# A two-block transformer in fp32 on one core: norms and the last units of each output projection taken by token tile

## The reference, cut to what matters

```python
def first_block(x, mem, ...):            # one even layer, one odd layer
    mem_n = rmsnorm(mem, mem_norm_g)
    h = even_layer(x, ...)               # rmsnorm, w_in, pool mixer + retention + memory attention, silu gate, w_out
    h = odd_layer(h, ...)                # rmsnorm, w_in, compressed/selected/window attention + memory attention, w_out
    return rmsnorm(h, final_g)

def second_block(x, p, ...):
    for i in range(2):
        h = rmsnorm_2(x, norm_mix[i])    # na_q, na_k, na_v, q_lat, kv_lat, k_rope, gate_a, gate_b = h @ w_in[i]
        ...                              # neighbourhood and latent attention
        x = x + merged @ w_out[i]
        x = x + expert_choice_moe(rmsnorm_2(x, norm_moe[i]), w_router[i], ...)   # 16 experts, 32 tokens each
        ple_gate = jax.nn.sigmoid(rmsnorm_2(x, norm_ple[i]) @ ple_gate_w[i])
        x = x + ple_gate * (p[i] @ ple_w[i])
    return rmsnorm_2(x, norm_final)

def rmsnorm(x, g):
    return x * lax.rsqrt(jnp.mean(x * x, axis=-1, keepdims=True) + 1e-6) * g
```

## Time and profile before

| | us |
|---|---|
| median of 3 runs | 2079.78 |
| the profiled execution, its own time | 2083.16 |
| its span | 2081.3 |
| PE busy | 1683.0 |
| PE weight loads busy | 1245.7 |
| DVE busy | 610.6 |
| ACT busy | 496.0 |
| POOL busy | 161.7 |

### The profile page before, as it was taken

One profiled execution on the slowest core, in us unless ns is written; L12 is line 12 of the kernel. 1 busy time (PEld: TensorE's weight loads), 2 busy tenths in 40 slices (PEclk: granted clock), 3 DMA queues, 4 the chain that ended last, 5 costly groups with the idle time before them and its releaser, 6 DMA issues. The chain is left out here.

```text
span 2081.3 us, 30041 instructions
## 1 busy us (share of the span) xinstructions
PE 1683.0 (81%) x12816; PEld 1245.7 (60%) x12816; DVE 610.6 (29%) x884; ACT 496.0 (24%) x884; POOL 161.7 (8%) x170
## 2 busy tenths in 40 slices
PE   7999999998799998866575756899998666757656
PEld 6999899997698777432232323887875232323225
DVE  2645444577344434000000001644342000000004
ACT  3434234455243331000000002432321000000003
POOL 0014000010031010000000001210100000000002
PEclk9999999999999999998899897999998898989997
DMA  8454649332453417899999998544238999999992
GB/s 286 146 167 143 191 143 308 111 102 83 140 147 116 162 53 317 370 426 426 424 426 427 425 427 334 156 123 166 87 155 353 424 427 425 426 426 428 426 419 92
DMA packets 173169, 563.66 MB, mean 271 GB/s; under 512 B 12745, under 2 KB 127327, under 8 KB 140172
## 3 DMA queue, kind: packets, MB, share of 16 engines
q1 hardware_dynamic: 165168, 552.05, 68.6%
q10 hardware_dynamic: 7900, 10.13, 1.5%
HBM read 561.08 MB, written 5.23 MB: 272 GB/s over the span
## 5 line engine op out<-in xcount | busy, mean ns | idle before, releaser
L1357 PE MATMUL bank<-ring,big 128*32 128x256 f32 x3840 | 279.7, 443 | 187.5 <-DMA ring<-in_moe_w 187.4
L886 PE MATMUL bank<-big_r,ring_r 128*128 128x256 f32 (+1 forms) x2880 | 362.4, 287 | 0.2 <-issue 0.2
L886 PEld LDWEIGHTS bank<-big_r,ring_r 128*128 128x128 f32 (+1 forms) x2880 | 353.7, 189 | 1.6 <-issue 1.2
L1357 PEld LDWEIGHTS bank<-ring,big 128*32 128x32 f32 x3840 | 146.5, 124 | 327.4 <-issue 285.7
L1755 DVE TENSOR_TENSOR ring_r<-ring,ring_r 128x2048 fp32r<-128x2048 f32 (+2 forms) x112 | 246.8, 2210 | 184.6 <-ACT ring_r L1439 183.2
L1479 ACT ACTIVATE big<-bank 128x512 f32<-128x512 f32 (+2 forms) x186 | 87.8, 490 | 542.8 <-PE bank L861 335.6
L1439 ACT ACTIVATE ring_r<-ring 128x2048 fp32r<-128x2048 f32 (+2 forms) x116 | 208.5, 1806 | 25.1 <-issue 12.4
L1378 PE MATMUL bank<-ring,big 128*32 128x512 f32 x1024 | 136.8, 628 | 76.5 <-DMA ring<-in_moe_w 59.5
L886 PE MATMUL bank<-ring_r,big_r 128*128 128x256 f32 (+3 forms) x1440 | 181.3, 287 | 1.9 <-POOL ring_r L2175 1.9
L886 PEld LDWEIGHTS bank<-ring_r,big_r 128*128 128x128 f32 x1440 | 178.3, 199 | 3.8 <-POOL ring_r L2175 2.7
L861 PE MATMUL bank<-big 128*128 128x128 f32 (+5 forms) x634 | 111.7, 309 | 70.1 <-ACT big L1429 32.5
(11 more groups left out here) (180 smaller groups left out, 1329.5 us busy)
## 6 DMA issues: line engine op xcount, KB each, us to landing
ring<-in_moe_w SPq DMA_DIRECT2D x120, 2048.0 KB, 23.7
ring<-in_moe_w SPq DMA_DIRECT2D x128, 1024.0 KB, 24.9
ring<-in_w_in SPq DMA_DIRECT2D x30, 1024.0 KB, 5.3
ring<-in_od_w_in SPq DMA_DIRECT2D x22, 1024.0 KB, 5.3
big<-in_moe_w SPq DMA_DIRECT2D x8, 2048.0 KB, 13.3
ring<-in_ev_w_in SPq DMA_DIRECT2D x11, 1024.0 KB, 11.0
ring<-in_ev_w_in SPq DMA_DIRECT2D x12, 768.0 KB, 4.5
ring<-in_od_cmp_w SPq DMA_DIRECT2D x8, 1024.0 KB, 8.4
```

The costliest lines, as they stand in the source:

```text
L886: ins = unit[0].mark(mm(dst, lhsT, rhs, start=start and n == 0, stop=stop and n == len(terms) - 1))
L1357: ins = mm(banks[5 + up][32 * j:32 * j + 32, 0:256], xg[:, k, q, :], wv[:, r, 256 * j:256 * (j + 1)], start=k == 0, stop=k == KC - 1)
```

## The change

There are five parts.

1. **Output projections.** Of each, the last four units (`LAST`) are done for token tile 0, all four, and then for token tile 1. DVE adds tile 0 into x, and its norm runs, while PE is at tile 1. The transposes of tile 0 stand between the units of tile 1 (`first_T`). A unit that is kept for its second tile (`hold`) counts `begun` up only there (`release`). The rounded halves of the gated rows (`g_high`) move to other places in SBUF.
2. **Norms.** Sums, roots, scalings, transposes and high and low parts go by token tile, each with semaphores of its own.
3. **The start of the second block.** One pass forms both norms: DVE multiplies x by `final_g` into `yb`, ACT sums the squares of x and of `yb`, POOL forms both factors (`double_norm`). The layer begins with the `nav` units, which have tokens on the output partitions and so can go by token tile (`values_start`). The unit's low weights are waited for late (`tile_rest`).
4. **The router.** Raw rows of x are transposed and multiplied by the gains, and the exponential takes the norm's factor as its scale. The rows for the gather are scaled afterwards on ACT, in an order in which the gather reads 128 columns in a row.
5. **Embedding gates.** Each evacuation is 512 columns of one token tile in place of 256 columns of both; all four `pg` units are kept for both tiles (`embed_gates`). The unit whose low part POOL makes is `pg` 3 in place of `pg` 1. The output is stored by tile.

Second output projection, PE, before: L1112 is a matmul of `out_proj`, L1070 to L1074 the values of head 11, L861 the transposes, L886 the first projection of layer 0.

```diff
+ODD = (proj("o_mk", 0) + [("T1", 2)] + proj("o_mk", 1) + proj("o_mv", 0) + [("uT", 2)] + proj("o_xq", 0, 1) + proj("o_mv", 1)
        + attention(MH, proj("o_gate", 6, 7) + proj("o_kc", 0) + proj("o_vc", 0) + proj("o_ks", 0))
...
+            k = out.index(("proj", "o_gate", 5))
+            out.insert(k + 1, ("outu", 1, 0))
+            out.insert(out.index(("NT", NH - 2)) + 1, ("outu", 1, 1))
...
+_first = [e for e in LAYER_PLAN if e[0] == "split"][:2]
+LAYER_PLAN = _first + [e for e in LAYER_PLAN if e not in _first]
+LAST = 4
...
+                def hold(s):
+                    s.first = False
+                    return s
+
+                def release(s):
+                    s.first, s.step = True, 2
+                    return s
...
+            def tile_T(t, src):
+
+                for half in range(2):
+                    for k in range(4):
+                        c = (4 * half + k) * P
+                        ins = tr(banks[4 + 2 * t + half][:, k * P:(k + 1) * P], src[:, t, c:c + P])
+                    ins.then_inc(uT_psum, 1)
...
+                    if i < n - LAST:
+                        tile(U, i, 0), tile(U, i, 1)
+                    else:
+                        if held:
+                            U.hold()
+                        held.append(U)
+                        tile(U, i, 0)
+                for k, U in enumerate(held):
+                    if k:
+                        U.release()
+                    if k == (3 if j == 1 else 2):
+                        first_T(l, j)
+                    tile(U, n - LAST + k, 1)
...
+            def tile_product(bank, c0, U, l, j, t, fresh, chunk_waits):
...
+                for k in range(KC):
+                    if chunk_waits:
+                        tile_ready(l, j, t, k)
+                    for x_ in (uTh_r, uT_r):
+                        ins = U.mark(mm(dst, x_[:, k, toks], hi[:, k, :], start=fresh and k == 0 and x_ is uTh_r,
+                                        stop=False, skip_group_check=True))
+                return ins
...
+            def tile_rest(bank, c0, U, t):
+
+                lo, hi = U.parts(256)
+                pe.wait_ge(*U.low)
+                for k in range(KC):
+                    ins = mm(bank[:, c0:c0 + 256], uTh_r[:, k, t * P:(t + 1) * P], lo[:, k, :], start=False,
+                             stop=k == KC - 1, skip_group_check=True)
+                return ins
...
+            def values_start(l):
+
+                held = []
+                for t in range(TT):
...
+                    for i in range(2):
+                        if t == 0:
+                            held.append(Unit(l, ("nav", i), late=True))
...
+                            if i:
+                                held[i].hold()
...
+                            bank = bank_of(l, "nav", i)
+                            if i:
+                                held[i].release()
+                        tile_product(bank, t * T, held[i], l, 0, t, t == 0, i == 0)
+                        ins = tile_rest(bank, t * T, held[i], t)
+                        if t:
+                            ins.then_inc(proj_done, 1)
...
+            def embed_gates(l):
+
+                held = []
+                rows_T(l, 2, 0)
+                for i in range(4):
+                    t, p = i // 2, i % 2
+                    if i == 1:
+                        rows_T(l, 2, 1)
+                    if i == 3 and l + 1 < LAYERS:
+                        rows_T(l + 1, 0, 0)
+                    bank = wait_bank(l, "pg", i)
+                    for n in (2 * p, 2 * p + 1):
+                        if t == 0:
+                            held.append(Unit(l, ("pg", n), late=True))
...
+                                held[n].hold()
+                        elif n:
+                            held[n].release()
+                        tile_product(bank, (n % 2) * T, held[n], l, 2, t, n % 2 == 0, p == 0 and n == 0)
+                        if t:
+                            ins = tile_rest(bank, (n % 2) * T, held[n], t)
+                    if t == 0:
+                        for n in (2 * p, 2 * p + 1):
+                            ins = tile_rest(bank, (n % 2) * T, held[n], t)
+                    ins.then_inc(proj_done, 1)
...
+                            ins = mm(banks[4 + 2 * (k // 4)][:, (k % 4) * P:(k % 4 + 1) * P], u[:, t, k * P:(k + 1) * P],
                                      onehot[:, t].rearrange("p q s -> p (q s)"), start=t == 0, stop=t == TT - 1)
...
+                        act.wait_ge(x_ready, 6)
+                        tile_ss(0, x[:, 0, :], lss)
+                        act.wait_ge(norm_ss[0], norm_at(None, 3) + 1)
+                        act.wait_ge(y_ready, 1)
+                        tile_ss(0, yb[:, 0, :])
+                        split(0, *EARLY[1])
+                        tile_scale(0, 0, 0, yb[:, 0, :])
+                        tile_high(0, 0, 0, layer_gains(0))
+                        act.wait_ge(x_ready, 8)
+                        tile_ss(1, x[:, 1, :], lss)
+                        act.wait_ge(norm_ss[1], norm_at(None, 3) + 1)
+                        act.wait_ge(y_ready, 2)
+                        tile_ss(1, yb[:, 1, :])
...
+                act.wait_ge(x_ready, 4 * out_at(l, 2) + 2)
+                tile_ss(0, x[:, 0, :])
+                tile_raw(l, 0, gl[:, 8:])
+                act.wait_ge(x_ready, 4 * out_at(l, 2) + 4)
+                tile_ss(1, x[:, 1, :])
+                tile_raw(l, 1, gl[:, 8:])
+                evacuate(l, *PLE_W[0][1:])
...
+                    A(aff[:, t, :], banks[3][:, t * NE:(t + 1) * NE], ACT.Exp, bias=rt[:, 6 + t:7 + t],
+                      scale=rstd[:, t:t + 1], accum_out=rt[:, 2 + t:3 + t]).then_inc(rt_exp, 1)
+                for t in range(TT):
+                    A(u[:, t, :].rearrange("p (i r q) -> p i q r", i=2, r=4),
+                      x[:, t, :].rearrange("p (i q r) -> p i q r", i=2, r=4), ACT.Copy,
+                      scale=rstd[:, t:t + 1]).then_inc(u_ready[t], 1)
...
+                        add_out(None, 1, 0)
+                        gained(0)
+                        final_rows(0)
+                        split(0, *EARLY[1])
+                        tile_parts(0, 0, 0, layer_gains(0))
+                        add_out(None, 1, 1)
+                        gained(1)
+                        tile_scale(0, 0, yb[:, 1, :])
+                        final_rows(1)
...
+                tile_ss(x[:, 1, :])
+                tile_parts(l, 2, 0, gl[:, 16:])
+                split(l, "pg", 1)
+                split(l, "pg", 2)
+                tile_parts(l, 2, 1, gl[:, 16:])
+                more = l + 1 < LAYERS
+                evacuate(l, "pg", 0)
+                if more:
+                    split(l + 1, *EARLY[0])
+                evacuate(l, "pg", 1)
+                evacuate(l, "pg", 2)
+                if more:
...
+            def double_norm(t):
+
+                c = slice(t, t + 1)
+                pool.wait_ge(norm_ss[t], norm_at(None, 3) + 1)
+                steps.link(g.tensor_scalar(lms[:, c], lss[:, c], 1.0 / D, EPS, ALU.mult, ALU.add))
+                g.tensor_tensor(lrstd[:, c], lms[:, c], neghalf[:, 0:1], ALU.pow).then_inc(norm_rstd[t], 1)
+                pool.wait_ge(norm_rstd[t], norm_at(None, 3) + 1)
+                pool.wait_ge(norm_ss[t], norm_at(0, 0) + 1)
+                steps.link(g.tensor_tensor(ms[:, c], ss[:, c], lrstd[:, c], ALU.mult))
+                steps.link(g.tensor_tensor(ms[:, c], ms[:, c], lrstd[:, c], ALU.mult))
+                steps.link(g.tensor_scalar(ms[:, c], ms[:, c], 1.0 / D, EPS, ALU.mult, ALU.add))
+                steps.link(g.tensor_tensor(ms[:, c], ms[:, c], neghalf[:, 0:1], ALU.pow))
+                g.tensor_tensor(rstd[:, c], ms[:, c], lrstd[:, c], ALU.mult).then_inc(norm_rstd[t], 1)
```

435 lines of the change are left out of this document (256 added, 179 removed).

## The result

| | before | after |
|---|---|---|
| median of 4 runs, us | 2080.57 | 2049.07 |
| lowest to highest | 2075.74 to 2083.79 | 2044.10 to 2052.04 |
| the profiled execution, own time | 2083.16 | 2051.12 |
| its span | 2081.3 | 2049.3 |
| PE busy | 1683.0 | 1650.9 |

The ratio is 0.9846, 95% interval 0.9830 to 0.9863: 31.5 us faster. The forecast was 2048, range 2038 to 2065.

What follows compares the result with a forecast made beforehand. The weight stream bounds the expert phases, PE's own work the rest, where only its holes can be won. Gains of 5.5 + 2.1 + 11.2 + 0 + 8.9 + 4.1 = 31.8 us give 2048 us, range 2038 to 2065.

Steps and rivals of the forecast that it cites:

- Places 3 and 5: Routers of both layers (T: output projection's start): later first expert load and shorter logits path cancel, 0 us.
- Rival A: Expert phases: the stream's late start is not given back in either layer, 17 us lost, 2065 us; chance 0.08.
- Place 2(c): Second output projection's end to first layer 0 products: kept half units hide the by-tile norm chain, 11.2 us gained.
- Place 2(b): Second output projection, head 11's values and unit 7: waits around the values go, 2.1 us gained.
- Place 2(a): Second output projection's start: low parts made before head 11's scores, unit 0 at 504.8, 5.5 us gained of 8.06.
- Place 4: Experts to layer 1: by-tile norms shorten both norm holes, first product 5.5 us after the experts; 8.9 us gained.
- Place 6: Kernel's end: last embedding gates start by tile, 1.9 us, and a shorter store tail, 2.2 us; 4.1 us gained.
- place 1: First output projection: the odd layer's norm was already hidden and stays hidden by tile, 0 us.
- B: Rival: DVE and ACT become the bound in the holes, halving gains at 2(c) and 4; 2058 us, chance 0.10.
- C: Rival: POOL's split of `pg` 3 blocks DVE for 3 us; 2051 us, or 2054 with the last layer; chance 0.08.
- D: Rival: held units stop SP's loads 8.5 us at five places or more, so the kernel is slower, 2091 us; chance 0.04.
- E: Rival: weights' low parts, not norms, end the holes, so by-tile norms bring nothing at 2(c) and 4; 2068 us, chance 0.04.

Runs made afterwards that it cites:

- the control: The changed kernel unedited, timed again on the same chip as follow-up runs: median 2047.46 us of 5 runs, ratio 0.9828 against the kernel before.
- the first of the two strided runs: The changed kernel with the gather reading every fourth column again and ScalarE scaling rows in plain order; single execution, own time 2049.95 us.

## Why the prediction came out right

**Places 3 and 5, the routers: right, and for the reason given.** The load went out at T + 15.4 (I had 14.65), the stream's idle time was 8.8 us before (8.5), and the phase ended as before to 0.4 us. The first expert stood at T + 47.4, not 49: without the gather the path to it is 3.7 us shorter, where I had 4.2, and the gather, which I counted as nothing, took 5.33 us for 7.74. The run with two kept units shows what the sum of 0 was made of: release the ring as before, and 6.2 us a layer come in. Rival A needed the idle time to stay; it went.

**Place 2(c): right; 10.7 for 11.2.** Beside the matmuls of the projection and of the products I foresaw 3.4 us: measured about 3.5, with 0.8 of transposes at 553.83 and 2.7 at 564. The products themselves took 0.4 us longer than before. Without kept units 8.5 us come back.

**Place 2(b): 2.1 for 2.1.** From unit 0's start to the projection's end, tile 0's transposes left out, 3.9 us were gained. 1.8 of them are the clock's, at units 0 and 1; the rest is head 11's values and the waits around them.

**Place 2(a): the mechanism half right, 3.8 for 5.5.** I saw the 2.5 us at head 10's values (2.76) and took unit 0 to wait for nothing but them, at 504.8. It started at 507.88. One thing was missing from the term: PE may not write to the projection's PSUM banks before VectorE has read head 11's scores, and that read now stands behind two splits. It is what I had as the lower bound, 3.0, "if head 11's steps, late by another split, come back to PE". PE also took 4.05 us for values that take 2.2, at a granted clock of 0.50 after its wait, but this cost nothing: in the three profiles where they took 2.2, PE waited for the same read. The order is worth 4 us, not 5.5. The clock gave some back: unit 0 and 1 took 12.13 us for 13.94, which no term foresaw. So the place as a whole, 18.5 for 18.8, is right in part by luck.

**Place 4: 10.7 for 8.9, and partly luck.** The first product came 5.4 us after the experts, as worked out (5.5). In twelve profiles with the same code here it came after 4.8 to 7.2 us in layer 0, and after 7.2 in the control. One part of that is where the count starts: the last expert's eight matmuls took 1.99 us in the control and 3.65 here. The other part is an encounter that the prediction didn't see. By tile, GpSimd forms tile 0's root while VectorE sums tile 1's squares (L1898, two inputs in SBUF), and whichever begins first holds the other up. Here GpSimd was first, by 0.06 us; in the run with `pg` 1 on GpSimd VectorE was:

```profile
1269.29 0.54 POOL L2396 TENSOR_TENSOR big<-big 128x1 f32<-128x1 f32 x1
1269.35 1.23 DVE L1898 CUSTOM_DVE_ANT_0 big<-big 128x1024 f32<-128x1024 f32 x1
```

```profile
1268.63 1.22 DVE L1898 CUSTOM_DVE_ANT_0 big<-big 128x1024 f32<-128x1024 f32 x1
1268.68 1.57 POOL L2396 TENSOR_TENSOR big<-big 128x1 f32<-128x1 f32 x1
```

An operation on a single column took 1.57 us for 0.54, and ScalarE's scaling of tile 0 waited for it. Of the 24 starts of the gates in the twelve profiles (two layers each), 18 have one of the root's two steps held, for 0.5 or 1.0 us. No run tests an order that avoids it. Counted from the start of the last expert's eight matmuls, the place takes 59.7 us before and 48.7 to 50.0 in the twelve, so 9.7 to 11.0 are gained in each of them. The transposes' wait and the chain of the second norm cost less than the 1.5 us set aside.

**Place 6: 6.0 for 4.1.** The tail after the last product was 9.0 us for 11.8, 2.8 where I had 2.2. The start was put at 1.9. The first product came 4.2 us sooner (5.5 after the last expert for 9.7), and the gates then took 1.0 longer, tile 1's transposes included: 3.2.

**Left out.** The start of the program: two norms stand there with nothing to hide them, and by tile GpSimd makes two roots one after the other. The first transposes begin at 13.94 for 13.54, the second ones at 27.2 for 25.2. In the other executions they began between 25.4 and 28.0, as the 32 matmuls before them took 7.17 to 9.54 us, so most of it is the clock's. And place 1 cost 0.9, cause open. Against these two stood more gain at 4 and 6; that the forecast met the time to 1 us owes something to that.

**Rivals.** B (queues halve the gains): 2(c) and place 4 kept theirs. C (GpSimd's split of `pg` 3 shuts VectorE out): it happened, at another operation and for less. VectorE in the changed kernel, and below it GpSimd:

```profile
1275.38 5.01 DVE L1957 TENSOR_TENSOR ring_r<-ring,ring_r 128x2048 fp32r<-128x2048 f32 x2
...
1283.30 2.13 DVE L2045 SCALAR_TENSOR_TENSOR big<-big 128x512 f32<-128x512 f32 x1
```

```profile
1271.45 4.58 POOL L2422 TENSOR_TENSOR ring_r<-ring,ring_r 128x2048 fp32r<-128x2048 f32 x1
1278.90 5.98 POOL L2422 TENSOR_TENSOR ring_r<-ring,ring_r 128x2048 fp32r<-128x2048 f32 x1 [2.87 <-ACT ring_r L1575]
```

GpSimd's split stretched from 4.58 to 5.98 until VectorE's ended at 1280.39, and then VectorE's gate operation stood until 1284.88: 2.13 us for 0.68. That fits the exclusion told of in the prediction. PE waited 0.85 us at 1293.13 at the end of that queue, 3 us were feared. In layer 0 of the twelve profiles the gate operation took 2.1 to 2.2 us in three, and PE waited 0.85, 0.92 and 0.99 us there; in the nine others it took 0.69 to 0.98, and PE did not wait. So the two go together, though no edit tests it. D (slower): its stalls never came, PE's waits name no DMA in the PE-bound stages. E: the norm's waits did end the holes.

**Signs that were wrong.** Unit 0's start and the first expert's are told of above. PE's busy time was to stay within 1%; it fell by 1.9%, 1683.0 to 1650.9. Nearly all of that is the gather, which the prediction put at nothing because it lay in a hidden stretch. Its 256 matmuls are booked with 61.9 us before and 33.6 after, 28.3 of the 32.1. With the gather alone put back (the first of the two strided runs) it is 61.9 again, and PE is busy for 1676.2. In the expert phase DMA sets the pace, so this work was saved and no time won: a busy sum tells nothing of time where the engine is not the limit.

## What to carry to other kernels

When a stage is bound by a stream of weights, look at what releases its first load, not only at what its first consumer waits for: here a shorter path and a late release cancelled within a microsecond, and releasing early without giving up the short path won 12 us more. When a wait is named after one producer, ask what else must be true at that point (a PSUM bank to be free, here), or the next producer in the queue takes its place. When a step is cut in two, look at which other engine now works beside each half: here VectorE's sum and GpSimd's root met on the critical path. Read small effects between two events near the edit; whole times of one code differed by more than the effect.

## What the hardware showed beyond that

- Behind a hole PE's work often ran at half speed. Head 10's first values took 1.19 us for 0.69 after the wait of 2.76, at a granted clock of 0.50; eight transposes took 1.97 for 1.03 after one of 4.19, and the 16 products behind them 3.71 for 2.08. In another execution the same values took 0.67 after 2.81 us, and the fall came one step later. In all, PE's work behind the hole took 1.9 us longer in the first case and 2.6 in the second.
- The clock dips in long busy stretches, too: in 613 to 633 us PE was busy for all 20 us, and 0.74 of full speed was granted in one execution; in the matching window of another, 0.83. The same code took 191.8 and 196.4 us from `nav` to the projection.
- 32 gather matmuls with every fourth column as the stationary operand took 7.73 us, at a granted clock of 0.58, of 0.72 and of 1.00 alike. With 128 columns in a row they followed the clock: 3.84 us at 1.00, 5.2 to 5.5 at 0.68 to 0.72, 6.2 to 6.7 at 0.54 to 0.59. So it was not the clock that held the strided ones.
- VectorE and GpSimd, each with two inputs in SBUF, take turns: 7.03 us for VectorE's two splits that take 4.58 alone. A 128x1 operation of GpSimd is held just as a long one is: 1.57 us for 0.54.
